# Modulation products of a two-block transformer: weights standing in place of rows, other places for them, the first norm ahead of them, softplus batched by function

## The reference

```python
cond = silu(c)                                    # 1 x 1024
for layer in range(2):
    mod = cond @ mod_w[layer] + mod_b[layer]      # 1024 x 6144
    sh1, sc1, g1, sh2, sc2, g2 = split(mod, 6)
    h = rms_norm(x, mix_norm_g[layer]) * (1 + sc1) + sh1
    mix = even_mixer(h, ...) if layer == 0 else odd_mixer(h, ...)
    x = x + g1 * mix
    h = rms_norm(x, ffn_norm_g[layer]) * (1 + sc2) + sh2
    x = x + g2 * moe(h, router_w, ..., 16 experts)
```

## Time and profile before

| | |
|---|---|
| time, median of 3 runs (lowest to highest) | 2345.51 us (2342.64 to 2348.91) |
| the profiled execution: its time, its span | 2345.21 us, 2343.4 us |
| mean granted clock of PE | 0.95 of 2.4 GHz |
| busy over the span | PE 90%, PEld 74%, DVE 55%, ACT 48%, POOL 48% |
| first product of the even mixer | 66.80 us |
| first transpose of norm(1), ahead of moe(0) | 302.05 us |
| first gather of moe(0) | 323.75 us |
| the products of `mod_w` in the odd mixer begin | 774.93 us |
| first transpose of norm(3), ahead of moe(1) | 874.77 us |

### The profile page before, as it was taken

One profiled execution on the slowest core, in us unless ns is written; L12 is line 12 of the kernel. 1 busy time (PEld: TensorE's weight loads), 2 busy tenths in 40 slices (PEclk: granted clock), 3 DMA queues, 4 the chain that ended last, 5 costly groups with the idle time before them and its releaser, 6 DMA issues.

```text
span 2343.4 us, 28178 instructions
## 1 busy us (share of the span) xinstructions
PE 2108.5 (90%) x11453; PEld 1733.0 (74%) x11453; DVE 1282.1 (55%) x1470; ACT 1115.6 (48%) x1130; POOL 1116.8 (48%) x466
## 2 busy tenths in 40 slices
PE   4886879999988878999998999988999999988998
PEld 0742467777768357777776999777998999767997
DVE  2745356666666545666666545565445545464454
ACT  1415346666654335666665334544344434544343
POOL 0400138777773024777876445423444445423453
PEclk8998979999998988999999999989999999989999
DMA  6454637787773653787876455523455455523553
GB/s 234 156 187 146 216 107 278 272 280 271 283 269 121 218 201 126 276 281 270 281 273 217 154 206 180 175 89 121 168 188 172 153 207 180 175 74 126 178 180 117
DMA packets 209010, 457.35 MB, mean 195 GB/s; under 512 B 8784, under 2 KB 20712, under 8 KB 208872
## 3 DMA queue, kind: packets, MB, share of 16 engines
q1 hardware_dynamic: 203904, 448.89, 55.6%
q10 hardware_dynamic: 4968, 6.54, 0.9%
HBM read 454.35 MB, written 1.05 MB: 194 GB/s over the span
## 4 chain that ended last, share of the span: by engine, by line
PE 67%; DVE 11%; ACT 9%; DMA 6%; issue 4%; POOL 3%; ACTq 0%; DVEq 0%; POOLq 0%; SPq 0%
PE bank L272 65%; DMA raw<-in_ex_w 4%; ACT pair1h L546 3%; ACT pair2h L546 2%; DVE arena L1096 2%; DVE pair1l L561 1%; DVE arena L1088 1%; PE bank L1726 1%; ACT pair0h L546 1%; POOL pair1l L553 1%; POOL pair2l L553 1%; DVE pair0l L561 1%; DVE xgl L1088 1%; DVE pair2l L561 1%; DVE xres L1096 0%
## 5 line engine op out<-in xcount | busy, mean ns | idle before, releaser
L553 POOL TENSOR_TENSOR pair1l<-raw,pair1h 128x512 fp32r<-128x512 f32 x126 | 362.9, 2880 | 421.8 <-ACT pair1h L546 421.7
L553 POOL TENSOR_TENSOR pair2l<-raw,pair2h 128x512 fp32r<-128x512 f32 x126 | 342.8, 2721 | 325.7 <-ACT pair2h L546 325.5
L553 POOL TENSOR_TENSOR pair0l<-raw,pair0h 128x512 fp32r<-128x512 f32 x127 | 341.6, 2689 | 313.2 <-ACT pair0h L546 313.1
L561 DVE TENSOR_TENSOR pair1l<-raw,pair1h 128x1536 fp32r<-128x1536 f32 x126 | 230.3, 1828 | 241.7 <-ACT pair1h L546 241.2
L561 DVE TENSOR_TENSOR pair2l<-raw,pair2h 128x1536 fp32r<-128x1536 f32 x126 | 230.8, 1832 | 229.9 <-ACT pair2h L546 229.6
L561 DVE TENSOR_TENSOR pair0l<-raw,pair0h 128x1536 fp32r<-128x1536 f32 x127 | 234.6, 1847 | 221.2 <-ACT pair0h L546 220.5
L546 ACT ACTIVATE pair0h<-raw 128x2048 fp32r<-128x2048 f32 x127 | 243.0, 1914 | 206.6 <-PE bank L272 185.0
L546 ACT ACTIVATE pair2h<-raw 128x2048 fp32r<-128x2048 f32 x126 | 241.2, 1915 | 196.5 <-PE bank L272 144.9
L546 ACT ACTIVATE pair1h<-raw 128x2048 fp32r<-128x2048 f32 x126 | 241.0, 1913 | 195.4 <-PE bank L272 156.8
L272 PE MATMUL bank<-hTh,pair0h 128*128 128x256 f32 x592 | 169.5, 286 | 7.9 <-DVE arena L1088 5.6
L272 PE MATMUL bank<-hTh,pair0l 128*128 128x256 f32 x592 | 168.9, 285 | 0.0
(11 more groups left out here) (286 smaller groups left out, 5130.4 us busy)
## 6 DMA issues: line engine op xcount, KB each, us to landing
raw<-in_ex_w SPq DMA_DIRECT2D x192, 1024.0 KB, 5.6
raw<-in_mod_w SPq DMA_DIRECT2D x48, 1024.0 KB, 5.2
raw<-in_ffn_w_gate SPq DMA_DIRECT2D x44, 1024.0 KB, 5.1
raw<-in_ffn_w_up SPq DMA_DIRECT2D x44, 1024.0 KB, 5.0
raw<-in_ffn_w_down SPq DMA_DIRECT2D x44, 1024.0 KB, 4.8
raw<-in_w_in SPq DMA_DIRECT2D x20, 1024.0 KB, 5.1
raw<-in_ev_in_w SPq DMA_DIRECT2D x10, 1024.0 KB, 5.2
raw<-in_od_in_w SPq DMA_DIRECT2D x8, 1024.0 KB, 5.0
```

The source lines that it names most:

```text
L553: e.tensor_tensor(lo[:, 0:cut], raw[:, 0:cut], hi[:, 0:cut].bitcast(F32), ALU.subtract).then_inc(S("lo_pool"), 1)
L561: e.tensor_tensor(lo[:, cut:], raw[:, cut:], hi[:, cut:].bitcast(F32), ALU.subtract).then_inc(S("lo"), 1)
```

## The change

- The products of the modulation are turned round: blocks of 128 x 128 of `mod_w` stand as weights and `condT`, one column, is streamed. 32 products per half (4 blocks of columns times 8 of rows) instead of 8. The result is in columns; the rows on ACT, the transposes on PE, `SUMMED` with its work on DVE, and `cbc` are gone.
- The gates, too, come as columns (`gcol`). DVE makes diagonals of them (`dgate`, eight instructions for two halves), PE multiplies these with ones (`gate_rows`, two products), ACT copies the result to `gbc`.
- Places (`UPTO`): four halves in `start` behind the transposes of the first norm, four behind the scores of the attention, two behind the sums R, two behind its output, two behind the residual of the even mixer, two in the router of moe(0), six in the odd mixer, two behind its residual.
- x is brought first on ACT's queue, and the first norm's squares and transposes come ahead of the products.
- Norms are transposed in four pairs of chunks in place of eight chunks.
- `ev_out_w` and `od_out_w` are split by input rows: the half whose input is ready first is multiplied first, into banks 4 to 7, and these are added to later.
- Softplus: Abs of three tiles, Exp of the three as one; the same for the other three; then Ln of both. 
- The convolution is in other places: 5 taps up to k, 9 ahead of the softplus sums, 2, 2, 3, and the rest behind the split of the output weights.

The diff, cut to what the prediction speaks of.

The plan and the places:

```diff
+MODS = (((0, 0), (0, 1)), ((0, 3), (0, 4), (1, 0), (0, 2)), ((1, 1), (0, 5)), ((1, 3), (1, 4), (1, 2)), ((1, 5),))
+UPTO = {"start": 4, "z": 8, "R": 10, "o": 12, "x1": 14, "m0": 16, "odd": 22, "x3": 24}
...
-    mod(0, 0)
-    mod(0, 1)
+    mods(0)
     square("ev_in_w", (0,), 0, 5)
-    for l, v in EVEN_MODS:
-        mod(l, v)
-    square("ev_out_w", (0,))
+    mods(1)
+    parts("ev_out_w", (512, 0))
+    mods(2)
     moe(0)
```

ACT, the gates' rows and the softplus:

```diff
+            def gate_rows(g0):
+                for g in (g0, g0 + 1):
+                    l, v, half = MOD_HALVES[GATES[g]]
+                    e.wait_ge(S("gate_row"), g + 1)
+                    e.activation(gbc[:, v // 5, half * 512:(half + 1) * 512], banks[row_bank(g)][:, :], ACT.Copy
+                                 ).then_inc(S("gate"), 1)
...
+                for par in range(2):
+                    p3 = slice(3 * par, 3 * par + 3)
+                    for i in range(3 * par, 3 * par + 3):
+                        e.wait_ge(*V("even_z", i + 1))
+                        ins = e.activation(L[:, i, :], banks[i][:, :], ACT.Abs)
+                    own.did(ins)
+                    own.see()
+                    own.did(e.activation(L[:, p3, :], L[:, p3, :], ACT.Exp, scale=-1.0))
+                own.see()
+                for par in range(2):
+                    p3 = slice(3 * par, 3 * par + 3)
+                    e.activation(L[:, p3, :], L[:, p3, :], ACT.Ln, bias=1.0).then_inc(S("even_ln"), 1)
```

DVE, the columns and the end of the even mixer:

```diff
+            def mods_to(point):
+                for q in range(done[0], UPTO[point]):
+                    l, v, half = MOD_HALVES[q]
+                    h4 = slice(4 * half, 4 * half + 4)
+                    o = gcol[:, v // 5, h4] if q in GATES else modc[:, l, {0: 0, 1: 1, 3: 2, 4: 3}[v], h4]
+                    e.wait_ge(S("used"), W.last("mod_w", (l,), v * D + half * 512) + 1)
+                    ins = tt(o, banks[mod_bank(q)][:, 0:4], c_modb[:, l, v, h4], ALU.add)
...
+                conv(3)
+                split_to(out(512, 0))
+                mods_to("o")
+                gate_diagonals(0)
+                split_to(out(512, 1))
+                conv(31)
                 e.wait_ge(*V("even_mean", 1))
```

PE, the products and the end of the even mixer:

```diff
+            def mods_to(point):
+                for q in range(made[0], UPTO[point]):
+                    l, v, half = MOD_HALVES[q]
+                    b = banks[mod_bank(q)]
+                    e.wait_ge(*V("cond", 1))
+                    if q >= 2:
+                        e.wait_ge(S("mod"), q - 1)
+                    for r, i, k, views in pieces("mod_w", (l,), D, v * D + half * 512, 512):
+                        for f in range(4):
+                            for c in range(k):
+                                ins = mm(e, b[:, f:f + 1], views[0][:, c, f * 128:(f + 1) * 128], condT[:, r + c:r + c + 1],
+                                         r + f + c == 0, r + c == KC - 1)
                         ins.then_inc(S("used"), 1)
...
+                mods_to("o")
+                part("ev_out_w", 512, 0, True, False)
+                gate_rows(0)
+                e.wait_ge(S("gate"), 2)
+                part("ev_out_w", 512, 1, True, False)
                 e.wait_ge(*V("even_conv", 1))
...
-                residual("ev_out_w", V("even_ul", 1))
-                norm(1)
+                e.wait_ge(*V("even_ul", 1))
+                for nh in range(2):
+                    part("ev_out_w", 0, nh, False, True)
+                mods_to("x1")
+                norm(1, UPTO["x1"])
```

More of the change, by code:

```diff
@@ L108, in mod, with mods, parts @@
             by_cols("mod_w", (l,), D, v * D + half * 512, 512, False)
+    def mods(stage):
+        for l, v in MODS[stage]:
+            mod(l, v)
+    def parts(name, order):
+        for r in order:
+            for half in range(2):
+                plan.append(((name, (0,), r, half * 512), True, 4, 512))
     def square(name, idx, c0=0, n=2):
@@ L145, in weight_plan @@
     plan.append((("gates",), True, 16, 128))
-    for l, v in ODD_MODS:
-        mod(l, v)
-    square("od_out_w", (0,))
+    mods(3)
+    parts("od_out_w", (0, 512))
+    mods(4)
     moe(1)
@@ L671, in x_rms, with norm_x @@
                 ins.then_inc(S("x_sq"), 1)
-            def norm(j, split):
+            def norm_x(j):
                 x_rms(j)
@@ L770, in even @@
[L770 to L779 removed]
+                projected(1024, qs, 0, S("even_q"))
@@ L1165, in residual @@
+            def residual(stage, name, r, gate, gates):
                 for nh in range(2):
-                    at = W.last(name, (0,), nh * 512)
+                    at = W.where[name, (0,), r, nh * 512]
                     split_to(at)
                     e.wait_ge(S("used"), at + 1)
+                    e.wait_ge(S("gate"), gates)
                     for th in range(2):
@@ L1211, in conv @@
                                 taps[c] = own.did(ins)
-                taps = [0] * 4
-                def between(k):
-                    for _ in range(EVEN_AT[k][1]):
-                        mod_half(q[0])
-                        q[0] += 1
-                    conv(EVEN_AT[k][0])
+                    cur[0] = min(cur[0] + n, 31)
                 ev = lambda c0: W.last("ev_in_w", (0,), c0)
+                out = lambda r, nh: W.where["ev_out_w", (0,), r, nh * 512]
                 split_to(ev(512))
@@ L1787, in norm @@
[L1787 to L1796 removed]
+            made = [0]
@@ L1798, in turn, with part @@
+            def part(name, r0, nh, start, stop):
+                i, k, views = take(name, (0,), r0, nh * 512)
+                for th in range(2):
+                    for c in range(k):
+                        ins = mm3(e, banks[4 + 2 * nh + th][:, :], [x[:, r0 // 128 + c, th * 128:(th + 1) * 128] for x in catT],
+                                  [x[:, c, :] for x in views], start and c == 0, stop and c == k - 1)
+                ins.then_inc(S("used"), 1)
             def turn(t):
@@ L1809, in turn @@
                     ins.then_inc(S("turned"), 1)
-            def residual(name, ready):
-                for nh in range(2):
-                    if nh == 0:
-                        e.wait_ge(*ready)
-                    tok_major(catT, name, (0,), nh * 512, (4 + 2 * nh, 5 + 2 * nh))
             def start():
```

558 lines of the change are left out of this document (225 added, 333 removed).

## The result

The changed kernel takes 2453.91 us (median of 4, 2450.01 to 2460.89), the kernel before 2344.07: ratio 1.0473, interval 1.0436 to 1.0511. It is slower, as forecast, by 110 us where 138 were summed. The profiled execution took 2457.28 us (span 2455.5), against 2345.21 (span 2343.4).

A forecast was written before the change was run, and what follows sets the result against it. PE was taken to bound the kernel. Terms of +18.2 (start), +39.9 (even mixer), +26.0 (router), +40.1 (odd mixer) and +14 (experts) sum to 138.2 us on 2345.21, giving 2483 us, range 2445 to 2510.

The forecast's parts named there:

- Clock and cost of a half: New modulation products: clock not raised, lost after some 4 us; a half costs 13.8 us at 1.2 GHz, bounds 12.2 to 13.8.
- 4 us given back: Modulation halves: a stretch entered at full clock was to cost 4 us less than at 1.2 GHz.
- Rivals 1 and 2: Products keep 2.4 GHz, 2330 us, chance 0.11; or clock kept where high, not raised where low, 2371 us, 0.05.
- rival 3: Experts lose their full lead, 11 us twice, and no stretch gets 4 us back: 2510 us; chance 0.04 with slower.
- Rival 1: Standing products keep 2.4 GHz or load no slower at 1.2; a half 7.0 us, total 2330 us, faster; chance 0.11.
- Start: Start up to the even mixer's first product: products from 22.3, four halves 55.2 us, end at 85.0 for 66.80, +18.2 us.
- Even mixer: Even mixer's first product to norm(1): 275.1 us against 235.25, +39.9.
- place B: Even mixer after its output halves: DVE splits weights before the gates' columns and taps, so the mean starts 33.5 us later.
- Router: Router of moe(0): two halves at low clock, 27.6 us, covering a PE wait of 1.55 us: +26.0 us.
- Odd mixer: Odd mixer from first modulation product to norm(3): six halves at low clock, 914.9 against 874.77, +40.1 us.
- place C: Odd mixer ahead of its output: DVE does columns and diagonals before the recurrence, so PE idles 10.9 us and starts low.
- Experts: Experts of both layers: fewer split and raw pieces ready, 0 to 11 us a layer, 7 taken, +14 us together.

The follow-up runs named there:

- Experiment 2: Changed kernel with each modulation product streaming 128 equal columns instead of 1: 2328.07 us; changed kernel with the row form of products restored: 2336.33 us.
- the kernel of 128 columns: Changed kernel with each modulation product streaming 128 equal columns of the conditioning in place of 1, same weight loads and order: 2328.07 us, ratio 0.9924.
- experiment 4: Against the kernel of 128 columns: softplus batching undone 2341.61 us, first norm's transposes back behind the halves 2325.00; against the changed kernel: batching undone 2456.95.
- the kernel before with its 64 bytes: Kernel before with 64 unused bytes of SBUF ahead of `rows`, so every tile behind lies 64 bytes further: 2316.03 us, ratio 0.9872.
- experiment 1: 64 unused bytes of SBUF added to the kernel before: 2316.03 us; to the changed kernel: 2485.10; ahead of the pair buffers alone in the kernel before: 2323.44.
- The best kernels here: The kernel of 128 columns with even and odd mixers' DVE work reordered: 2277.36 us; the same with the first two start halves taken earlier: 2275.77.

## Why the prediction was right, and where not

- **Clock and cost of a half: right.** Where PE comes to the halves at full clock, they begin at 1.00 and fall to 0.50 with PE busy throughout, as said; the four behind the scores, where it comes at 0.50, stay there. In the router the clock rose within the first microsecond of the halves and fell again; whether they raised it or the transposes ahead of them did, no run shows. The two halves R (the row, and windows in it), and the two in the router:

```profile
219.70 22.33 PE L272 MATMUL bank<-condT,raw 128*128 128x1 f32 x128
220.00:221.00 1.00, 1.00 (x11) 1.00 (x10) 1.00 (x3) 0.38 (x1) 0.00 (x0) 1.00 0.00 0
226.00:227.00 1.00, 1.00 (x7) 1.00 (x6) 0.00 (x0) 0.00 (x0) 0.00 (x0) 0.50 1.02 389
378.29 24.20 PE L272 MATMUL bank<-condT,raw 128*128 128x1 f32 x128
```

  The forecast's "4 us given back" came from no row; it was 0.7 us (o) to 5.1 us (R) a place. The four halves behind the scores, which got none, take 54.77 us, 13.7 each (13.8 said). Experiment 2 shows that the few streamed columns are the reason: with more streamed the same loads go at 2.4 GHz. The page "TensorE: Matmul & The Clock Gate" of the Trainium skill, table "Why this matters for your kernels", promises full clock to an engine kept busy; here 10.00 of 10 us busy stand at 0.50. Its section "LDWEIGHTS (loading the stationary operand)" has the load independent of the clock; here the pair of load and product takes 0.213 us at one level and, with 128 columns streamed, 0.113 at the other (14.45 us for 128). Rivals 1 and 2 fall on this, rival 3 on the experts' 6.5 and 7.0 us. Rival 1's time needs a word: its "40 us of modulation less" is 56 by its own halves (its total uses the 56), and the kernel of 128 columns, which has its clock, takes 2328 for its 2330. That is luck: against the kernel before, start, even and odd mixer (64.8, 219.1 and 108.3 us) stand at -2, -16 and +8 there, not -9, -25 and -8, and the second block's 14.5 us of other pace helps to hide it.
- **Start: +20.8 for +18.2, right.** The four halves take 54.6 us for 55.2 and begin 2.5 us later than said; PE waits 8.2 us for the norm's low part. The norm ahead was charged nothing, and in the kernel of 128 columns it is worth nothing (experiment 4). The granted clock is no witness here, the length of the row is:

```profile
24.80 54.61 PE L272 MATMUL bank<-condT,raw 128*128 128x1 f32 x256
30.00:31.00 1.00, 1.00 (x6) 1.00 (x7) 0.00 (x0) 0.00 (x0) 0.00 (x0) 1.00 0.00 0
```

- **Even mixer and place B: right in total.** The wait is there (timeline of the changed kernel, PE):

```profile
309.30 3.78 PE L272 MATMUL bank<-arena,cst 128*128 128x256 f32 x8 [12.52 <-DVE arena L1070]
...
327.33 0.80 PE L272 MATMUL bank<-pair0h,catTh 128*128 128x512 f32 x1 [8.06 <-DVE catTl L1062]
956.24 0.76 PE L272 MATMUL bank<-pair2h,catTh 128*128 128x512 f32 x1 [11.77 <-issue]
```

  The mean starts 34.4 us behind the last product of "o" at 274.9; 33.5 were said. ("R", "o", "x1", "m0" and "x3" are the places of `UPTO`.) One term was too low: 4 us were taken off the four halves behind the scores, which came at low clock already (0.53 from 150 to 151 us, inside the scores), so they took 54.8 us for 51.2, and the scores 8.0 for 5.2. Most later terms came out 0.4 to 1.7 us shorter than said and make up for it, which is in part luck.
- **Router: +23.7 for +26.0.** The term charged the full 27.6; the two halves took 24.2 (row above), because the clock rose as they began, which the forecast had ruled out (0.62 from 378 to 379 us, 1.00 in the three behind, 0.50 again from 384 to 385).
- **Odd mixer: +42.7 for +40.1.** The third row above is place C, 11.8 us of idle for 10.9. The profile names no releaser; DVE's list does, with diagonals and recurrence ahead of the split that the product at 956.24 needs:

```profile
944.59 2.67 DVE L1066 TENSOR_SCALAR dgate<-cst,gcol 128x128 f32<-128x128 f32 x8
...
954.38 1.75 DVE L563 TENSOR_TENSOR pair2l<-raw,pair2h 128x1536 fp32r<-128x1536 f32 x1
```

- **Experts: 6.5 and 7.0 for 7 each.** Right, though the cause (lead of split and raw pieces) was not taken apart.
- **The step that failed** is the one that had no term: "the expert and feed-forward stages are the same code". They are, but not at the same addresses, and that is -28.3 us, nearly the whole gap between 2483 and 2454. At like addresses the sum fits: the changed kernel is 137.9 us above the kernel before with its 64 bytes (2453.9 and 2316.0), where 138.2 were summed. With its pair buffers 128 bytes from their old place it takes 2485.1, at rounds a little longer than the old ones; the changed kernel exactly at the old place was not run.
- **"Worth nothing" of the softplus** holds for this kernel (2457 for 2454), because its halves are slow. The reason given, four halves as cover, is wrong: the cover is two, and at full clock the batching is worth 13.5 us.

So of the change at its own address, 126 us net are the column form's clock, by the runs of experiment 2. What is left, places, norm and batching, is 12 us against the kernel before with the same 64 bytes (2328 to 2316), 7.8 of them, in the profiled executions, in the second block (experiment 1), and 39 us the other way (2277) once DVE's order follows PE's. The best kernels here (2277 and 2276) are 67 and 68 us, 2.9%, faster than before, 28 of them from the address.

## What to carry to other kernels

Of a product with few streamed columns on a large standing block, ask whether the engine's clock survives it; look at the granted clock of a like stretch first. Where the load sets the pace, more streamed columns can be cheaper than one, as here. Work placed "beside" other work is covered only as far as the banks between the two engines reach, here two of four halves, and only if each engine's own list has its part there in time. And a change of layout is a change to every stage behind it: time the kernel with its tiles moved by the same bytes before an untouched stage is called equal.

## What was not expected of the hardware

- 64 bytes of SBUF offset take 28 us off one kernel (of 2344) and add 31 to the other (of 2454): the same 240 products at full clock take 33.94 us at the old place and 33.94 to 34.23 at a third. At the place between them they take 32.77 or 33.62, and both lengths occur in one execution.
- 128 streamed columns instead of one halve the time of a load-bound product, 0.213 to 0.113 us, because the granted clock is 1.00 instead of 0.50.
- The record of the granted clock cannot be trusted ahead of its first change: the first four halves of the changed kernel stand at 1.00 while they take 54.61 us, the pace of 0.50.
